# A first RMSNorm whose factor is applied to the results in PSUM instead of the operand

## The chip, the cores and the metric

The kernel is written in Bass for one core of one Trainium2 chip, with each engine's instruction stream written by hand. The metric is the device time of that core in microseconds, as the median of several executions.

## What is computed

Two blocks on x of 1 x 256 x 2048, all in float32. The part of the first that matters here, with `rmsnorm(x, g) = x * rsqrt(mean(x*x) + eps) * g` over the last axis:

```python
h = rmsnorm(x, norm_mix_pre)
proj = h @ w_in
xr, yr, q, k, v, g_rnn, g_attn = split(proj)   # 2048, 2048, 2048, 256, 256, 2048, 2048
xr = rg_lru(causal_depthwise_conv(xr, conv_w, conv_b), ...)   # gates, decay, scan over time
y_rnn = xr * gelu(yr)
q, k = rope(q), rope(k)
y_att = sliding_window_sink_attention(q, k, v, attn_sinks)
mix = sigmoid(g_rnn) * (y_rnn @ w_rnn_proj) + sigmoid(g_attn) * (y_att @ w_attn_proj)
x = x + rmsnorm(mix @ w_out, norm_mix_post)
h = rmsnorm(x, norm_mlp_pre); x = x + rmsnorm(relu(h @ w_mlp_up)**2 @ w_mlp_down, norm_mlp_post)
```

The second block has a norm, a wide input product, a differential attention, an S5 state-space branch and an output product.

## The kernel before, in words

**Products.** Each float32 product is three matmuls in fp32r: with the operand split into h_hi and h_lo and the weights into w_hi and w_lo, they are hi·hi, lo·hi and hi·lo, summed in PSUM. SP streams the weights in groups of two k-tiles by 512 columns (512 KB) into `raw`, a ring of four slots. ScalarE makes w_hi of a group (`split_hi`, L556), VectorE w_lo = raw - w_hi (`split_lo`, L1014). Eight groups are a unit, which fills `acc[u % 2]`, half of PSUM. `unit` on TensorE has two forms: by token (L1722 to L1724) and by feature (L1714 to L1717).

**Order.** Every engine walks the same list of units. `steps` on ScalarE and VectorE splits group j + 3 (`LEAD`) and then calls the hooks of step j: the unit's other work stands in these hooks, so a hook that waits holds up the splits behind it. `split_hi` of a group waits until TensorE is done with the group three before it (`pe_used`); SP's load waits for `lo_ready`; an accumulator comes free by `acc_free`.

**Start.** SP issues one DMA for x (L319), twelve for rows of parameters (L330), which land in `stg`, and then the weights. TensorE transposes the parameter rows (L1761, L1762), ScalarE copies them to `pt1` and `pt2`. ScalarE squares x (L581), VectorE and GpSimd make rstd of it (`mean_square`, POOL L432). For each of four chunks of 512 columns ScalarE writes x times rstd into `stg` (`h_chunk`, L594), TensorE transposes `stg` into `tps` (`turn`, L1737), ScalarE makes h_hi with the gain as scale (`evac_hi`, L574), VectorE h_lo (`evac_lo`, L1033). The first unit computes k and v (`U_KV`). Beside it and the next, VectorE computes the rotary angles, cosines, lambda, softplus and the rotation of k.

**Then** comes a loop of units for q and xr, in turn, with the attention in their hooks. xr goes from `acc` to `slab_d` on ScalarE (`xr_out`, L666).

**Recurrent units** (four, by feature, product yr; chunk c of 512 features in each). In their hooks: the gates (ScalarE L699, L702), decays (L712, L716) and a root (L721); on VectorE the decay (L1265 to L1267), the convolution of the next chunk (L1236, L1238) and the scan (`states`, L1272 to L1275). Behind a unit's steps ScalarE takes gelu of the accumulator (L729) into `slab_d`. In the next unit VectorE multiplies it with the scan's result (`y_product`, L1249) once `acc_free` says so; ScalarE makes the high part (`y_high`, L689), VectorE the low (`y_low`, L1254). POOL's queue loads the gate weights (L442).

**Mix units** follow: tanh of the gates from PSUM with scale 0.5 (L743), four times two units. The first block's second norm and the MLP are untouched. In the second block the norm's factor is already applied to results: rstd is turned into a row over all partitions by TensorE (`rstd_row`), copied (L825), and used as an operand (L1467, L1474).

In the names of tiles, `slab_dg_f` is `slab_d`, `slab_i_f` holds x, and `side` and `tps` are the two other parts of PSUM.

## Time and profile before

| | |
|---|---|
| median of 3 runs | 2541.09 us (2540.49 to 2541.24) |
| span of the profiled execution | 2539.6 us |
| its own time beside the span | the median lies 1.5 us above the span |
| TensorE busy | 2384.5 us, 94% |
| VectorE busy | 1483.3 us, 58% |
| ScalarE busy | 1206.1 us, 47% |
| GpSimd busy | 162.7 us, 6% |
| DMA | 410 MB, mean 161 GB/s |

The busy shares are means over the whole span. TensorE is nearly full overall, so the places to look at are those in which it is not, and there the waits tell which engine or transfer comes last. A "[idle <- releaser]" at a row's end is the time for which the engine stood before it and what ended that.

### The profile page before, as it was taken

What the parts mean: (1) busy time and instruction counts of PE and PEld (TensorE: products, weight loads), DVE (VectorE), ACT (ScalarE), POOL (GpSimd) and SP (SyncE); (2) the same over time, 40 slices, a digit from 0 to 9 for tenths busy, and PEclk for the clock granted to TensorE, in tenths of its full rate; (3) what the DMA queues carried; (4) which work ended last, traced back from release to release, by engine and by line L of the source; (5) the groups of instructions that cost most, each with busy time, mean ns of one, the idle gap of its engine ahead of it and who ended that gap; (6) DMA issues with size and microseconds to landing.
All of it is one profiled execution on the core that took longest, in us unless ns stands there. A gap on an engine that the chain in (4) does not pass through costs nothing.

```text
span 2539.6 us, 34016 instructions
## 1 busy us (share of the span) xinstructions
PE 2384.5 (94%) x11782; PEld 1962.7 (77%) x11782; DVE 1483.3 (58%) x1917; ACT 1206.1 (47%) x1746; POOL 162.7 (6%) x196
## 2 busy tenths in 40 slices
PE   5999888899999979999999999989999988898999
PEld 4888788888888868888888888879666657677887
DVE  3666557745454555545545555566778785665554
ACT  5444445544444444434444344354666754544443
POOL 2000000000000000000000000010433320010000
PEclk9999989999999989999999999999999998999999
DMA  5544324466666736666566666655333334445665
GB/s 178 162 132 125 114 86 132 153 195 190 190 191 191 255 127 191 187 195 188 186 189 189 191 188 188 191 151 174 107 108 99 107 108 125 140 140 156 185 189 166
DMA packets 209069, 410.00 MB, mean 161 GB/s; under 512 B 12960, under 2 KB 13248, under 8 KB 208192
## 3 DMA queue, kind: packets, MB, share of 16 engines
q1 hardware_dynamic: 206336, 398.64, 51.3%
q0 software_dynamic: 2624, 9.83, 1.3%
q8 instruction: 77, 1.26, 0.2%
q14 instruction: 32, 0.26, 0.0%
HBM read 406.33 MB, written 2.10 MB: 161 GB/s over the span
## 4 chain that ended last, share of the span: by engine, by line
PE 70%; issue 13%; DVE 8%; ACT 4%; POOL 3%; DMA 0%; SPq 0%; DVEq 0%; POOLq 0%; ACTq 0%
PE acc L1722 19%; PE acc L1724 19%; PE acc L1723 19%; PE acc L1714 3%; PE acc L1716 2%; PE acc L1717 2%; PE tps L1737 2%; DVE w_lo L1014 1%; PE side L1776 1%; ACT w_hi L556 1%; POOL k_t L474 1%; POOL t_low L473 1%; DVE stg L1238 1%; PE tps L1920 1%; DMA raw<-in_w_in_dram 0%
## 5 line engine op out<-in xcount | busy, mean ns | idle before, releaser
L1014 DVE TENSOR_TENSOR w_lo<-raw,w_hi 128x1024 fp32r<-128x1024 f32 x752 | 921.0, 1230 | 855.2 <-ACT w_hi L556 850.5
L556 ACT ACTIVATE w_hi<-raw 128x1024 fp32r<-128x1024 f32 x752 | 793.2, 1059 | 956.2 <-PE acc L1724 795.4
L1722 PE MATMUL acc<-w_hi,h_hi 128*128 128x512 f32 x1440 | 583.1, 405 | 22.9 <-DVE w_lo L1014 9.4
L1724 PE MATMUL acc<-w_hi,h_lo 128*128 128x512 f32 x1440 | 566.8, 394 | 0.0
L1723 PE MATMUL acc<-w_lo,h_hi 128*128 128x512 f32 x1440 | 566.5, 393 | 0.0
L1722 PEld LDWEIGHTS acc<-w_hi,h_hi 128*128 128x128 f32 x1440 | 274.2, 190 | 104.6 <-issue 33.4
L1724 PEld LDWEIGHTS acc<-w_hi,h_lo 128*128 128x128 f32 x1440 | 273.5, 190 | 59.6
L1723 PEld LDWEIGHTS acc<-w_lo,h_hi 128*128 128x128 f32 x1440 | 274.8, 191 | 52.8
L1722 PE MATMUL acc<-w_hi,slab_dg_r 128*128 128x512 f32 x768 | 299.4, 390 | 0.0
L1724 PE MATMUL acc<-w_hi,slab_dg_r 128*128 128x512 f32 x768 | 299.0, 389 | 0.0
L1723 PE MATMUL acc<-w_lo,slab_dg_r 128*128 128x512 f32 x768 | 298.8, 389 | 0.0
L1714 PE MATMUL acc<-h_hi,w_hi 128*128 128x256 f32 x768 | 225.5, 294 | 7.0 <-DVE w_lo L1014 7.0
L1716 PE MATMUL acc<-h_lo,w_hi 128*128 128x256 f32 x768 | 220.5, 287 | 0.0
L1717 PE MATMUL acc<-h_hi,w_lo 128*128 128x256 f32 x768 | 220.3, 287 | 0.0
L1723 PEld LDWEIGHTS acc<-w_lo,slab_dg_r 128*128 128x128 f32 x768 | 144.2, 188 | 29.9
L1724 PEld LDWEIGHTS acc<-w_hi,slab_dg_r 128*128 128x128 f32 x768 | 144.2, 188 | 29.8
L1722 PEld LDWEIGHTS acc<-w_hi,slab_dg_r 128*128 128x128 f32 x768 | 144.2, 188 | 29.8
L1714 PEld LDWEIGHTS acc<-h_hi,w_hi 128*128 128x128 f32 x768 | 150.7, 196 | 15.9 <-issue 15.6
L1716 PEld LDWEIGHTS acc<-h_lo,w_hi 128*128 128x128 f32 x768 | 150.8, 196 | 0.3
L1717 PEld LDWEIGHTS acc<-h_hi,w_lo 128*128 128x128 f32 x768 | 150.5, 196 | 0.0
L1722 PE MATMUL acc<-w_hi,slab_f_r 128*128 128x512 f32 x256 | 100.4, 392 | 0.0
L1724 PE MATMUL acc<-w_hi,slab_h_r 128*128 128x512 f32 x256 | 99.7, 389 | 0.0
(351 smaller groups left out, 2328.7 us busy)
## 6 DMA issues: line engine op xcount, KB each, us to landing
raw<-in_w_in_dram SPq DMA_DIRECT2D x328, 512.0 KB, 3.8
raw<-in_w_mlp_up_dram SPq DMA_DIRECT2D x128, 512.0 KB, 3.8
raw<-in_w_mlp_down_dram SPq DMA_DIRECT2D x128, 512.0 KB, 3.9
raw<-in_w_out_dram SPq DMA_DIRECT2D x64, 512.0 KB, 4.7
raw<-in_w_rnn_proj_dram SPq DMA_DIRECT2D x32, 512.0 KB, 4.2
raw<-in_w_attn_proj_dram SPq DMA_DIRECT2D x32, 512.0 KB, 4.8
raw<-in_w_proj_ssm_dram SPq DMA_DIRECT2D x16, 512.0 KB, 5.2
raw<-in_w_proj_att_dram SPq DMA_DIRECT2D x16, 512.0 KB, 4.4
```

The lines of the kernel that those rows point to most:

```text
L473: chain.link(pool.tensor_tensor(t_low[:, :], t_row, phi[:, 1, j:j + 1].broadcast_to([P, SEQ]), ALU.mult))
L474: chain.link(pool.tensor_tensor(f, f, k_round[:, j, :], ALU.subtract))
L556: nc.scalar.activation(w_hi[:, j % RING], raw[:, j % RING], ACT.Copy).then_inc(hi_ready, 1)
L1014: V.tensor_tensor(w_lo[:, j % RING], raw[:, j % RING], w_hi[:, j % RING].bitcast(F32), ALU.subtract)\
L1238: ins = V.scalar_tensor_tensor(xc4[:, m, late:], xr, w, xc4[:, m, late:], ALU.mult, ALU.add)
L1714: T.matmul(o, wh[:, c], hi[:, k, :], start=first and m % 2 == 0, stop=False, skip_group_check=True)
L1716: T.matmul(o, wh[:, c], lo[:, k, :], start=False, stop=False, skip_group_check=True)
L1717: ins = T.matmul(o, wl[:, c], hi[:, k, :], start=False, stop=last, skip_group_check=True)
L1722: T.matmul(o, hi[:, k, c], wh, start=first, stop=False)
L1723: T.matmul(o, hi[:, k, c], wl, start=False, stop=False)
L1724: ins = T.matmul(o, lo[:, k, c], wh, start=False, stop=last)
L1737: ins = T.transpose(tps[:, b * SEQ + t * P:b * SEQ + (t + 1) * P], stg[:, t, b * P:(b + 1) * P], ident[:, :])
```

## The change

h is no longer x·rstd·gain but x·gain, and rstd, one factor for each token, is applied to what comes out of PSUM.

- **Loads.** x comes in four DMAs of 512 columns (SP L338), alternating with the first three weight groups. The twelve parameter rows are issued from ScalarE's queue (L582).
- **Start.** TensorE transposes x itself as its chunks land, into two parts of PSUM in turn (`turn_x`), and ScalarE and VectorE evacuate with `x_high` (L595) and `x_low`. The squares follow in the hooks of steps 0 and 1 and rstd in the hook of step 2; the rotary hooks of ScalarE move back by one step, on VectorE cosines from 4 to 5.
- **k, q.** The cosines and sines are multiplied by rstd on VectorE, four small operations. **v** is copied in two with rstd as scale.
- **xr, yr.** They lie with tokens along the free axis. TensorE spreads rstd to a row in the second unit (hook 5), ScalarE copies it. xr leaves PSUM on VectorE, multiplied by the row. yr is multiplied by the row on VectorE behind the unit's steps (L1303), which frees the accumulator; gelu is taken in `slab_d` after it (L737), and `y_product` waits for `gelu_ready`.
- **Gates of the mix.** tanh takes half of rstd as its scale, one instruction for each half of the tokens.
- **POOL** starts the gate weights' loads when x's transposes are done (`tps_ready`).

SP at the start of the program; `raw` are the weights. Before:

```order
L319 DMA slab_i_f<-in_x_dram 128x2x2048
L330 DMA stg<-in_norm_mix_pre_dram 16x128
L330 DMA stg<-in_conv_w_dram 64x128
...
L330 DMA stg<-in_ssm_lambda_im_dram 32x128
L339 DMA raw<-in_w_in_dram 128x2x512 x4
```

Now:

```order
L338 DMA slab_i_f<-in_x_dram 128x2x512
L326 DMA raw<-in_w_in_dram 128x2x512
L338 DMA slab_i_f<-in_x_dram 128x2x512
L326 DMA raw<-in_w_in_dram 128x2x512
...
L326 DMA raw<-in_w_in_dram 128x2x512 [waits lo_ready] x4
```

The twelve rows have left SP, and x and the weights alternate.

VectorE from the scan of the second recurrent unit on. Before:

```order
L1275 SCALAR_TENSOR_TENSOR tmp<-tmp,slab_dg_f 128x256 [waits v_chain]
L1275 SCALAR_TENSOR_TENSOR tmp<-tmp,slab_dg_f 128x256 x3
L1014 TENSOR_TENSOR w_lo<-raw,w_hi 128x1024 [waits hi_ready] x2
L1249 TENSOR_TENSOR tmp<-slab_dg_f,tmp 128x1024 [waits y_ready,acc_free0]
L1014 TENSOR_TENSOR w_lo<-raw,w_hi 128x1024 [waits hi_ready]
```

Now (the row of rstd is called t_low here):

```order
L1287 SCALAR_TENSOR_TENSOR tmp<-tmp,slab_dg_f 128x256 [waits v_chain]
L1287 SCALAR_TENSOR_TENSOR tmp<-tmp,slab_dg_f 128x256 x3
L1005 TENSOR_TENSOR w_lo<-raw,w_hi 128x1024 [waits hi_ready]
L1303 TENSOR_TENSOR slab_dg_f<-acc,t_low 128x1024 [waits pe_used]
L1005 TENSOR_TENSOR w_lo<-raw,w_hi 128x1024 [waits hi_ready]
L1261 TENSOR_TENSOR tmp<-slab_dg_f,tmp 128x1024 [waits y_ready,gelu_ready]
L1005 TENSOR_TENSOR w_lo<-raw,w_hi 128x1024 [waits hi_ready]
```

The multiply stands between the two splits ahead of `y_product`, and waits for TensorE's end of the unit.

ScalarE at the same hand-over. Before:

```order
L556 ACTIVATE w_hi<-raw 128x1024 [waits pe_used,raw_landed2]
L729 ACT_TABLE_LOAD
L729 ACTIVATE slab_dg_f<-acc 128x1024 [waits pe_used]
L556 ACTIVATE w_hi<-raw 128x1024 [waits pe_used,raw_landed3]
L689 ACTIVATE slab_e_r<-tmp 128x1024 [waits y_ready]
```

Now:

```order
L549 ACTIVATE w_hi<-raw 128x1024 [waits pe_used,raw_landed2]
L737 ACT_TABLE_LOAD
L737 ACTIVATE slab_dg_f<-slab_dg_f 128x1024 [waits acc_free0]
L549 ACTIVATE w_hi<-raw 128x1024 [waits pe_used,raw_landed3]
L697 ACTIVATE slab_e_r<-tmp 128x1024 [waits y_ready]
```

gelu stands at its old place, but waits for VectorE's multiply instead of TensorE. The diff, cut to its core:

```diff
-            sp.dma_start(x_view, x_in).then_inc(x_landed, 16)
-            for rows, tile in ((FIRST_ROWS, 0), (SECOND_ROWS, 1)):
...
-                    sp.dma_start(stg[at:at + n, tile, 0:P], src).then_inc(rows_landed, 16)
...
-            unit(w_in, slice(o_k, o_k + NC), U_KV * S)
+            for c in range(NH):
+                at = slice(c * NC, (c + 1) * NC)
+                sp.dma_start(x_view[:, :, at], x_in[:, :, at]).then_inc(x_landed[c], 16)
+                if c < LEAD:
+                    load(w_in, slice(o_k, o_k + NC), 2 * c, U_KV * S + c, c)
+            for s in range(LEAD, S):
+                load(w_in, slice(o_k, o_k + NC), 2 * s, U_KV * S + s, s)
...
-                            pool.wait_ge(stg_ready, NH)
+                            pool.wait_ge(tps_ready, NH)
...
+            for rows, tile in ((FIRST_ROWS, 0), (SECOND_ROWS, 1)):
+                at = 0
+                for name, n in rows:
...
+                    act.dma_start(stg[at:at + n, tile, 0:P], src).then_inc(rows_landed, 16)
+                    at += n
 
             act.wait_ge(pt_ready, 1)
             nc.scalar.activation(pt1[:, :], tps[:, 0:P], ACT.Copy)
             nc.scalar.activation(pt2[:, :], tps[:, P:2 * P], ACT.Copy).then_inc(cols_ready, 1)
 
...
+            def x_high(c, t0, col):
+
+
...
+                for b in range(QPC):
+                    at = c * QPC + b
+                    ins = nc.scalar.activation(h_hi[:, at, :], x_bank(c, b), ACT.Copy, scale=col[:, at:at + 1])
+                ins.then_inc(tps_hi, 1)
...
+            def x_squares(c, first_x):
+                if first_x is None:
+                    act.wait_ge(x_landed[c], 16)
+                else:
+                    act.wait_ge(x_new, first_x + c + 1)
...
+                    ins = nc.scalar.activation(e_tok[:, t, c * NC:(c + 1) * NC], x_tok[:, t, c * NC:(c + 1) * NC],
+                                               ACT.Square, accum_out=ssq[:, t, c:c + 1])
...
                 act.wait_ge(ang_ready, 1)
...
-
+            def row_copy(index):
+                act.wait_ge(row_ready, index)
+                nc.scalar.activation(row[:, :], side[0][:, 0:SEQ], ACT.Copy).then_inc(row_copied, 1)
...
+            mix_gain = pt1[:, COL1["norm_mix_pre"]:COL1["norm_mix_pre"] + KT]
+            x_high(0, 0, mix_gain)
+            split_hi(None, 0, 0, 0)
+            split_hi(None, 0, 0, 1)
+            x_high(1, 0, mix_gain)
+            split_hi(None, 0, 0, 2)
+            hooks = {0: [lambda: x_squares(0, None), lambda: x_squares(1, None)], 1: [lambda: x_squares(2, None), lambda: x_squares(3, None)],
+                     4: [rotary_sines], 5: [exponentials]}
+            for c in range(2, NH):
+                x_high(c, 0, mix_gain)
+                steps(None, 0, U_KV * S, hooks, c - 1, start=c - 2)
+            steps(None, 0, U_KV * S, hooks, start=2)
+            unit_over(None, 0, U_KV * S)
             act.wait_ge(rstd_ready, 1)
-            first_unit(0, U_KV * S, pt1[:, COL1["norm_mix_pre"]:COL1["norm_mix_pre"] + KT],
-                       {3: [rotary_sines], 5: [exponentials]})
-            unit_over(None, 0, U_KV * S)
-            nc.scalar.activation(v_tok[:, :, :], tok(acc[0])[:, :, SEQ:2 * SEQ], ACT.Copy).then_inc(v_ready, 1)
+            for t in range(TT):
+                ins = nc.scalar.activation(v_tok[:, t, :], tok(acc[0])[:, t, SEQ:2 * SEQ], ACT.Copy, scale=rstd[:, t:t + 1])
+            ins.then_inc(v_ready, 1)
 
...
-                unit_over(i, 2 * S, (U_QX + 1 + 2 * c) * S)
-                settle()
-                nc.scalar.activation(slab_d[:, span(i, QPC, QPC * c, QPC), :], feat(acc[0]), ACT.Copy).then_inc(acc_free[0], 1)
...
-            steps(None, 0, U_QX * S, {5: [k_copy]})
+            steps(None, 0, U_QX * S, {3: [lambda: row_copy(1)], 5: [k_copy]})
...
-                beside_q[0] = [lambda: xr_out(i, 0)] + beside_q.get(0, [])
...
-                unit_over(None, 0, u * S)
-
-                nc.scalar.activation(slab_d[:, c * QPC:(c + 1) * QPC, :], feat(acc[u % 2]), ACT.Gelu_apprx_tanh)\
-                    .then_inc(acc_free[u % 2], 1)
+                act.wait_ge(acc_free[u % 2], u // 2 + 1)
+                at = slice(c * QPC, (c + 1) * QPC)
+                nc.scalar.activation(slab_d[:, at, :], slab_d[:, at, :], ACT.Gelu_apprx_tanh).then_inc(gelu_ready, 1)
             y_high(NH - 1)
 
 
...
-                    nc.scalar.activation(tmp[:, :, :], tok(acc[u % 2]), ACT.Tanh, scale=0.5).then_inc(acc_free[u % 2], 1)
+                    for t in range(TT):
+                        ins = nc.scalar.activation(tmp[:, t, :], tok(acc[u % 2])[:, t, :], ACT.Tanh, scale=half_rstd[:, t:t + 1])
+                    ins.then_inc(acc_free[u % 2], 1)
...
-            mean_square(1, 1)
...
+
+                dve.wait_ge(rstd_ready, 1)
+                chain.mark(V.tensor_scalar(half_rstd, rstd, 0.5, None, ALU.mult))
+                for t in range(TT):
+                    for b in (cosb, sinb):
+                        chain.mark(V.tensor_scalar(b[:, t, :], b[:, t, :], rstd[:, t:t + 1], None, ALU.mult))
 
                 dve.wait_ge(lam_landed, 160)
...
+            dve.wait_ge(cols_ready, 1)
+            x_low(0, H_X, mix_gain)
+            split_lo(None, 0, 0, 0)
+            split_lo(None, 0, 0, 1)
+            x_low(1, H_X, mix_gain)
+            split_lo(None, 0, 0, 2)
+            hooks = {2: [lambda: mean_square(NH, 1)], 3: [rotary_angles], 5: [cosines_and_lambda], 6: [softplus]}
+            for c in range(2, NH):
+                x_low(c, H_X, mix_gain)
+                steps(None, 0, U_KV * S, hooks, c - 1, start=c - 2)
+            steps(None, 0, U_KV * S, hooks, start=2)
+            dve.sem_inc(stg_ready, NH)
             dve.wait_ge(v_ready, 1)
...
+            def xr_out(i, c):
+                unit_over(i, 2 * S, (U_QX + 1 + 2 * c) * S)
+                rows_ = row[:, :].unsqueeze(1).broadcast_to([P, QPC, SEQ])
+                if i is not None:
+                    dve.wait_ge(row_copied, 1)
+                V.tensor_tensor(slab_d[:, span(i, QPC, QPC * c, QPC), :], feat(acc[0]), rows_, ALU.mult).then_inc(acc_free[0], 1)
+
...
+                    beside_q[0] = [lambda: xr_out(i, 0)] + beside_q.get(0, [])
...
+            xr_out(None, NH - 1)
...
-                dve.wait_ge(acc_free[(U_YR + c) % 2], (U_YR + c) // 2 + 1)
+                dve.wait_ge(gelu_ready, c + 1)
                 dve.wait_ge(y_ready, 2 * c + 1)
...
+                u = U_YR + c
+                unit_over(None, 0, u * S)
+                rows_ = row[:, :].unsqueeze(1).broadcast_to([P, QPC, SEQ])
+                V.tensor_tensor(slab_d[:, c * QPC:(c + 1) * QPC, :], feat(acc[u % 2]), rows_, ALU.mult).then_inc(acc_free[u % 2], 1)
             y_product(NH - 1)
...
             def turn_x(c, t0, first_x):
 
-                pe.wait_ge(x_new, first_x + c + 1)
-                pe.wait_ge(tps_free, t0 + max(c - 1, 0))
+                if first_x is None:
+                    pe.wait_ge(x_landed[c], 16)
+                else:
+                    pe.wait_ge(x_new, first_x + c + 1)
+                if t0 or c >= 2:
+                    pe.wait_ge(tps_free, t0 + max(c - 1, 0))
                 for t in range(TT):
...
+            def x_as_it_comes(c, t0, first_x):
+                pe.wait_ge(tps_free, t0 + c + 1)
+                if c < NH - 2:
+                    turn_x(c + 2, t0, first_x)
+
+            def rstd_row(index):
+
+                pe.wait_ge(rstd_ready, index)
+                for t in range(TT):
+                    ins = T.matmul(side[0][:, t * P:(t + 1) * P], rstd[:, t:t + 1].broadcast_to([P, P]), ident[:, :],
+                                   start=True, stop=True)
+                ins.then_inc(row_ready, 1)
+
+            for c in range(2):
+                turn_x(c, 0, None)
+            unit(None, 0, U_KV * S, 0, U_KV, h_hi, h_lo, before={4 * c // 2: [lambda c=c: x_as_it_comes(c, 0, None)] for c in range(NH)})
...
-            unit(None, 0, U_QX * S, 0, U_QX, h_hi, h_lo, hooks={9: [lambda: turn(None, 0, T_K)]})
+            unit(None, 0, U_QX * S, 0, U_QX, h_hi, h_lo, hooks={5: [lambda: rstd_row(1)], 9: [lambda: turn(None, 0, T_K)]})
```


## Rows read from the trace of the kernel before

**Rows 1.** Busy time by stretch of the span: TensorE, its loads, VectorE, ScalarE, GpSimd, clock, DMA

```profile
0.00:72.41 72.41, 39.46 (x166) 31.00 (x167) 32.88 (x93) 35.28 (x54) 16.82 (x36) 1.00 0.57 174
72.41:87.20 14.79, 14.79 (x70) 12.36 (x71) 8.25 (x7) 5.41 (x6) 0.00 (x0) 1.00 0.74 234
87.20:345.00 257.80, 241.15 (x1541) 209.94 (x1541) 153.65 (x347) 119.64 (x264) 0.00 (x0) 0.96 0.40 117
345.00:505.00 160.00, 144.06 (x973) 135.51 (x973) 113.31 (x148) 92.96 (x127) 5.76 (x8) 0.97 0.44 136
505.00:2539.60 2034.60, 1945.02 (x9037) 1573.85 (x9035) 1175.16 (x1324) 952.83 (x1297) 140.10 (x152) 0.98 0.55 168
```

**Rows 2.** Timeline of the start: start us, length us, engine, line, what, [idle before]

```profile
7.16 0.42 SPq L330 DMA_DIRECT2D stg<-in_ssm_lambda_im_dram  x1
...
14.16 0.45 PE L1762 MATMUL tps<-ident,stg 128*128 128x128 f32 x1 [14.16 <-DMA stg<-in_ssm_lambda_im_dram]
...
23.67 1.94 PE L1737 MATMUL tps<-ident,stg 128*128 128x128 f32 x8 [8.85 <-ACT stg L594]
...
27.25 1.66 DVE L1033 SCALAR_TENSOR_TENSOR h_lo<-tps,pt,h_hi 128x256 fp32r<-128x256 f32 x4 [3.69 <-ACT h_hi L574]
...
30.65 0.78 PE L1722 MATMUL acc<-w_hi,h_hi 128*128 128x512 f32 x1
...
34.21 0.63 PE L1724 MATMUL acc<-w_hi,h_lo 128*128 128x512 f32 x1
...
36.22 0.39 PE L1722 MATMUL acc<-w_hi,h_hi 128*128 128x512 f32 x1
...
47.31 1.66 DVE L1033 SCALAR_TENSOR_TENSOR h_lo<-tps,pt,h_hi 128x256 fp32r<-128x256 f32 x4 [3.58 <-ACT h_hi L574]
```

**Rows 3.** Timeline, VectorE's stream behind it and TensorE's wait for it

```profile
55.72 1.22 DVE L1014 TENSOR_TENSOR w_lo<-raw,w_hi 128x1024 fp32r<-128x1024 f32 x1 [1.42 <-ACT w_hi L556]
...
71.13 4.63 DVE L1014 TENSOR_TENSOR w_lo<-raw,w_hi 128x1024 fp32r<-128x1024 f32 x4 [0.15 <-DVE stg L1142]
...
72.41 0.50 PE L1722 MATMUL acc<-w_hi,h_hi 128*128 128x512 f32 x1 [1.55 <-DVE w_lo L1014]
```

**Rows 4.** Timeline of the recurrent units, second and third hand-over

```profile
392.62 1.22 DVE L1249 TENSOR_TENSOR tmp<-slab_dg_f,tmp 128x1024 f32<-128x1024 f32 x1
...
425.46 2.33 DVE L1014 TENSOR_TENSOR w_lo<-raw,w_hi 128x1024 fp32r<-128x1024 f32 x2
427.71 1.22 DVE L1249 TENSOR_TENSOR tmp<-slab_dg_f,tmp 128x1024 f32<-128x1024 f32 x1
...
414.79 1.02 ACT L729 ACTIVATE slab_dg_f<-acc 128x1024 f32<-128x1024 f32 x1
...
428.96 1.06 ACT L689 ACTIVATE slab_e_r<-tmp 128x1024 fp32r<-128x1024 f32 x1 [12.20 <-DVE tmp L1249]
...
451.50 0.55 PE L1714 MATMUL acc<-h_hi,w_hi 128*128 128x256 f32 x1 [3.43 <-DVE w_lo L1014]
```

**Rows 5.** DMA issues at 8.1, 8.6, 8.01, 8.53 and 9.06 us: KB, us to landing

```profile
raw<-in_w_in_dram SPq DMA_DIRECT2D x1, 512.0 KB, 11.8
...
raw<-in_w_in_dram SPq DMA_DIRECT2D x1, 512.0 KB, 12.6
...
slab_h_f<-in_lambda_k_dram POOLq DMA_DIRECT2D x1, 32.0 KB, 6.6
...
slab_h_f<-in_lambda_q_dram POOLq DMA_DIRECT2D x1, 32.0 KB, 8.0
...
slab_h_f<-in_lambda_k_dram POOLq DMA_DIRECT2D x1, 32.0 KB, 10.9
```

**Rows 6.** Groups by line, VectorE: the same multiply by the row, second block

```profile
L1474 DVE TENSOR_TENSOR stg<-acc,t_low 128x1024 f32<-128x1024 f32 x2 | 2.4, 1224 | 0.5 <-PE acc L1717 0.5
```

**Rows 7.** Timeline, TensorE's last wait behind the fourth recurrent unit

```profile
494.91 0.50 PE L1722 MATMUL acc<-w_hi,h_hi 128*128 128x512 f32 x1 [1.60 <-DVE w_lo L1014]
```

**Rows 8.** Busy time of the stretch 310 to 350 us, columns as in rows 1

```profile
310.00:350.00 40.00, 31.75 (x191) 29.30 (x190) 19.06 (x60) 14.30 (x33) 0.00 (x0) 0.79 0.17 45
```

More of the change, by code:

```diff
@@ L823, in _ @@
             steps(None, 0, G_U, start=2)
[L824 to L825 removed]
+            row_copy(2)
             steps(None, 0, G_U + S, {1: [s5_trig_]})
```

112 lines of the change are left out of this document (24 added, 88 removed).

## The prediction

> **What bounds the kernel now.** I read the time stretch by stretch first [rows 1]. From 505 us on TensorE is busy 1945.0 of 2034.6 us and the change touches only one ScalarE operation there, so the places to look at are the first 87 us and the stretch from 345 to 505 us. In the first 72.4 us TensorE is busy 39.5 us: that is where something can be won.
>
> The timeline of the start [rows 2] is a chain. The twelve parameter rows are issued on SP behind x, the last at 7.16 us, and TensorE's first two transposes start when they have landed, at 14.16 us. Then comes a chunk of x: eight transposes at 23.67, the end of its h_lo at 27.25 + 1.66 = 28.91, so 5.24 us for a chunk at the slow clock. Only after a second chunk's transposes does the first matmul start, at 30.65. Until 34.4 us matmuls follow each other every 0.43 us (a row of 0.63 us), later every 0.23 us (a row of 0.39 us): TensorE at 1.2 and then at 2.4 GHz, after a start from short bursts.
>
> From the last h_lo (47.31 + 1.66 = 48.97) VectorE is the bound [rows 3]: weight splits, rotary angles, lambda, softplus and the rotation of k stand in one stream, and TensorE's wait at 72.41 ends with the fourth group of the next unit, whose w_lo is the first of the four at 71.13. From 72.41 to 87.2 TensorE runs without a gap [rows 1], so what the end of that stream gains, the kernel gains.
>
> In the stretch from 345 us the four recurrent units are a ring of ScalarE and VectorE, not of TensorE [rows 4]. From one y_product (392.62) to the next (427.71) it is 35.1 us. TensorE works some 31.5 us of it and then waits for w_lo (3.43 us at 451.50). The ring: y_product, y_high on ScalarE (which had waited 12.20 us for it), splits, gates, decays, root, then VectorE's decay, convolution and scan, splits, y_product. The gelu at 414.79 stands outside it.
>
> **The start, part by part.** Removed from the path: the squares over all of x, the eight scalings of x into stg, and the wait of the first split and transposes for them. The transposes now need the parameter rows and x's chunk alone.
>
> When the rows land is the open term. They go out on ScalarE's queue, 12 at about 0.53 us each, so the last is issued near 7.1 us as before. In before, GpSimd's small transfers show what sharing costs [rows 5]: the one issued at 8.01 took 6.6 us, those at 8.53 and 9.06, which meet the 512 KB weight loads, took 8.0 and 10.9 us and landed at 16.5 and 20.0, while the loads issued at 8.1 and 8.6 landed at 19.9 and 21.2. A small transfer passed about once per load, not at once. Now eight such transfers (four of x, four of w) are issued by about 4.6 us. They take about 1.35 us each (19.9 to 21.2), with the small ones between them some 1.6 us: 1.5 + 8 x 1.6 = 14.3 us. Some eight of twelve rows have passed by then; the last four at 0.34 us each (twelve in 14.13 - 10.0 us behind x), and a landing, give 16 us. Bounds: 7.1 + 3.6 (the quickest load of the profile) = 10.7 us if they pass freely; 20 us if, like the transfer issued at 9.06, they take 10.9 us and more. I take 16, by the rows nearest to it. The Trainium skill (DMA: Bandwidth & Descriptors, Queues, rings and completion order) says the same: a DMA engine takes turns between the queues by packets of some 9 to 17 descriptors. It adds (Issuing engines are not separate DMA queues) that issuing from several engines saves only issue time, which speaks against this part; by it the rows land with the last of the eight transfers.
>
> From there: 1.5 us for two transposes and two copies (17.5); 5.24 us for chunk 0 (22.8); chunk 2's transposes, which now stand ahead of the unit, 1.9 us: first matmul at 24.7 us instead of 30.65. Two groups, 24 matmuls, take 5.5 us at 0.23 us each and about 1.2 us of slow clock (before: 2.2), chunk 3's transposes 1.0 us, its h_hi and h_lo 3.2 us: the last h_lo ends at 35.5 instead of 48.97, **13.5 us earlier**.
>
> VectorE's stream behind it took 72.3 - 48.97 = 23.3 us. It gains one w_lo of 1.15 us that used to stand ahead, 0.5 us of mean square, 0.85 us for half_rstd and the four scalings of cosine and sine, a wait of some 2.2 us for the w_hi that ScalarE now does behind squares of two chunks (3 us), 0.9 us of short waits, and loses the 1.4 us wait at 55.72: +4.2 us. So the matmul of 72.41 comes at 63.2 us: **the start gives 9.3 us**.
>
> At nothing: the transposes of rstd (0.3 us, while TensorE waits for VectorE anyway); the gate weights, now issued near 42 us (their unit is 300 us away); the split tanh of the mix units, 2 x 0.69 instead of 1.03 us, four times, covered by three groups of w_lo in stock (8 us); the v copy in two. If that cover were gone it would be 0.34 us each.
>
> **The xr copies** go from ScalarE (1.0 us) to VectorE (1.22 us, the same operation further on [rows 6]). In the loop VectorE is busy 153.65 of 257.80 us [rows 1] and the next user of that accumulator comes a unit later: zero. In the last unit the multiply stands ahead of the late `finish` calls, which wait for TensorE's products in any case: zero. If each did reach the path it would be 4 x 1.2 us.
>
> **The recurrent units.** Here the change adds to the ring. Before, gelu needed TensorE's unit alone, and was done 12 us before y_product. Now the multiply stands on VectorE behind the scan and the last split, since it is issued after them, and gelu, which waits for it, holds up ScalarE's next w_hi, on which VectorE's next w_lo waits, and behind that stands y_product. Before: w_lo, w_lo (2.25 us), y_product. After: w_lo 1.14, multiply 1.22, gelu 0.95, w_hi 1.07, w_lo 1.14 = 5.5 us. That is **+3.3 us** at each of three hand-overs. ScalarE's wait of 12.20 us hides none of it, because it ends with this same chain. At the fourth the w_hi stands behind y_high anyway: multiply and gelu alone, +2.2 us, and TensorE's wait at 494.91 is for what follows [rows 7]. Sum 3 x 3.3 + 2.2 = **+12.1 us**.
>
> **Sum:** -9.3 + 12.1 = +2.8 us. The profiled span of 2539.6 us becomes 2542.4; the median lies 1.5 us above that span, so 2541.1 + 2.8 = **2543.9 us**, slower by 0.11%. A measurement of this kernel can tell some 0.2%, 5.1 us, from no change.
>
> **Rivals.**
> 1. *The rows pass freely.* Landing at 10.7 us: the start gives 9.3 + 5.3 = 14.6, net -2.5: 2538.6 us. For: small transfers issued before 8 us took a steady 6.3 to 6.9 us. Against: the last two [rows 5].
> 2. *Slower: the rows are last of all.* Place: TensorE's first wait. If each turn of the engines costs 2 us, or the rows come after every load, they land at 20 us and the start gives 5.3: net +6.8, 2547.9 us. It decides from 18.4 us on (net +5.1).
> 3. *Slower: the clock joins the ring.* With some 8 us of waits in a unit of 38.4 us the granted clock could fall as it did at 310 to 350 us (0.79) [rows 8]. TensorE's 31.5 us were at 0.97 [rows 1], 30.5 at full clock, and become 38.6 at 0.79: the ring. At 0.70 they are 43.6, 5.2 us more in each of three units, net +18.4: 2559.5 us. It decides below 0.79.
> 4. *Faster: multiply and gelu fit into ScalarE's wait.* Net -9.3: 2531.8 us. It needs the multiply ahead of the scan, and the order of the code denies that.
> 5. *The change does not do what it says*: the first norm leaves the path only if the rows are not later than the norm was. They would have to land at 25 us.
>
> **How the numbers follow.** My forecast 0.50, rival 1 0.24, rival 2 0.13, rival 3 0.05, rival 4 0.05, others 0.03. Faster by over 0.2% (under 2536.0): rival 4 and the edge of rival 1, 0.09. Slower by over 0.2% (over 2546.2): rivals 2 and 3 and some, 0.18. Within: 0.73. The range runs from the low bound of the landing (rival 1) to its high bound (rival 2), 2538.0 to 2548.5, and leaves out 3, 4 and the rest.
>
> **What would show it.** First transposes at 16 us (10.7: rival 1; 20: rival 2); first matmul near 24.7; TensorE's last wait for w_lo of the second unit ending at 63. From y_product to y_product 38.4 us, with w_lo, multiply, gelu, w_hi, w_lo in a row ahead of it; 35.1 us would refute me. The stretch from 505 us unchanged within 1 us. I am wrong if the recurrent stretch grows by less than 8 us, or if the start is bound by x or w and not by the rows.

## The result, and the profile after

| | before | changed |
|---|---|---|
| median | 2540.49 us (9 runs, 2537.54 to 2543.27) | 2546.34 us (9 runs, 2545.19 to 2548.16) |
| ratio | | 1.0023, 95% interval 1.0013 to 1.0033 |
| span of the profiled execution | 2539.6 us | 2543.9 us |
| mean granted clock | 0.978 | 0.973 |

The change makes the kernel slower by 5.9 us of medians (0.23%), 4.3 us between the two profiled spans. The forecast was 2543.9 us, 2538.0 to 2548.5, and most likely no change that can be told. The time lies in the range, but a little beyond the 0.2% (2546.2 us) that counted as none, an outcome to which the forecast gave 0.18. What became of the two halves can be read well, because at each place the two traces can be compared in time.

Busy time of the changed kernel in the stretches of [rows 1], columns as there:

```profile
0.00:72.41 72.41, 50.10 (x221) 41.16 (x222) 39.34 (x104) 35.81 (x64) 17.71 (x36) 0.95 0.71 213
72.41:87.20 14.79, 13.86 (x96) 12.49 (x95) 10.49 (x14) 5.46 (x6) 0.00 (x0) 1.00 0.54 168
87.20:345.00 257.80, 239.87 (x1538) 208.62 (x1537) 161.41 (x361) 116.34 (x259) 0.00 (x0) 0.96 0.38 114
345.00:505.00 160.00, 136.09 (x887) 127.00 (x886) 105.09 (x130) 87.17 (x121) 5.77 (x8) 0.93 0.41 125
505.00:2543.90 2038.90, 1950.45 (x9053) 1578.29 (x9051) 1177.27 (x1325) 955.99 (x1307) 140.36 (x152) 0.98 0.54 168
```

TensorE is busy 10.6 us longer by 72.41 us than before, and 8.0 us less in the recurrent stretch. In each row "(x...)" is the number of instructions, and the last three columns are the granted clock, the busy share of the DMA engines and GB/s.

The start, the changed kernel's timeline (it answers to [rows 2, 3]):

```profile
7.09 0.63 ACTq L582 DMA_DIRECT2D stg<-in_ssm_lambda_im_dram  x1
...
15.57 0.45 PE L1766 MATMUL tps<-ident,stg 128*128 128x128 f32 x1 [15.57 <-DMA stg<-in_ssm_lambda_im_dram]
...
23.54 0.78 PE L1730 MATMUL acc<-w_hi,h_hi 128*128 128x512 f32 x1
...
32.96 1.66 DVE L1050 SCALAR_TENSOR_TENSOR h_lo<-side,pt,h_hi 128x256 fp32r<-128x256 f32 x4 [3.17 <-ACT h_hi L595]
...
57.23 0.80 PE L1730 MATMUL acc<-w_hi,h_hi 128*128 128x512 f32 x1 [2.68 <-DVE w_lo L1005]
...
85.74 0.92 PE L1795 MATMUL side<-k_c,slab_dg_f 64*128 64x128 f32 x4 [0.93 <-ACT slab_dg_f L650]
```

The last row is the attention's first scores; before, they came here:

```profile
96.34 0.92 PE L1776 MATMUL side<-k_c,slab_dg_f 64*128 64x128 f32 x4 [0.93 <-ACT slab_dg_f L635]
```

The parameter rows have landed at 15.57 us (16 forecast), the first matmul of the product starts at 23.54 (24.7), the last h_lo ends at 34.6 (35.5), and the first scores are 10.6 us earlier.

A hand-over between recurrent units in the changed kernel, VectorE, ScalarE and TensorE (before: [rows 4]):

```profile
418.50 1.20 DVE L1005 TENSOR_TENSOR w_lo<-raw,w_hi 128x1024 fp32r<-128x1024 f32 x1
419.62 1.22 DVE L1303 TENSOR_TENSOR slab_dg_f<-acc,t_low 128x1024 f32<-128x1024 f32 x1
422.91 1.22 DVE L1005 TENSOR_TENSOR w_lo<-raw,w_hi 128x1024 fp32r<-128x1024 f32 x1 [2.07 <-ACT w_hi L549]
424.05 1.22 DVE L1261 TENSOR_TENSOR tmp<-slab_dg_f,tmp 128x1024 f32<-128x1024 f32 x1
...
420.87 1.06 ACT L737 ACTIVATE slab_dg_f<-slab_dg_f 128x1024 f32<-128x1024 f32 x1 [13.05 <-DVE slab_dg_f L1303]
421.83 1.04 ACT L549 ACTIVATE w_hi<-raw 128x1024 fp32r<-128x1024 f32 x1
...
447.83 0.55 PE L1722 MATMUL acc<-h_hi,w_hi 128*128 128x256 f32 x1 [4.81 <-DVE w_lo L1005]
...
462.42 1.22 DVE L1261 TENSOR_TENSOR tmp<-slab_dg_f,tmp 128x1024 f32<-128x1024 f32 x1
```

Split, multiply, gelu, w_hi, split, y_product stand in a row as the forecast had them, and from one y_product to the next it is 38.37 us (38.4 forecast, 35.1 before). ScalarE still waits 13 us, now for the multiply and ahead of gelu. TensorE's granted clock does fall in this ring, to 0.67 over 405 to 415 us and 0.66 over 444 to 454 us, where the lowest such stretches of before read 0.81 to 0.87 (385 to 395, 415 to 424 and 444 to 454 us); TensorE's waits (4.81 us here) take it up, and the period stays.

The way out of the last recurrent unit, TensorE, and the clock behind its wait, in the changed kernel (before: [rows 7]):

```profile
489.92 0.50 PE L1730 MATMUL acc<-w_hi,h_hi 128*128 128x512 f32 x1 [1.32 <-DVE w_lo L1005]
...
496.88 0.66 PE L1730 MATMUL acc<-w_hi,h_hi 128*128 128x512 f32 x1 [3.95 <-DVE w_lo L1005]
497.35 0.63 PE L1731 MATMUL acc<-w_lo,h_hi 128*128 128x512 f32 x1
...
500.63 0.40 PE L1730 MATMUL acc<-w_hi,h_hi 128*128 128x512 f32 x1
```

```profile
496.80:500.00 3.20, 3.12 (x8) 2.44 (x9) 3.20 (x4) 1.43 (x2) 0.00 (x0) 0.54 0.57 166
```

The wait of 1.60 us has become 3.95, and behind it eight matmuls run at 1.2 GHz (0.43 us apart) and not at 2.4 GHz (0.23 us): 1.6 us that the forecast did not have. Before, the granted clock was 1.00 there. From the end of this wait to the first tanh of the mix it is 15.53 us, and was 13.93.

Put together, by how much later (+) or earlier (-) the changed kernel is at the same piece of work: first scores -10.6; fourth y_product (492.12 against 490.15) +2.0; first tanh of the mix (512.41 against 508.84) +3.6; last tanh (819.76 against 816.19, the first half of it in the changed kernel) +3.6; first multiply by a row in the second block (1705.43 against 1700.88) +4.6; end +4.3. From the first tanh to the end it is 0.7 us longer, within the 1 us that the forecast allowed for that stretch. The first y_product (385.67 against 392.62) is at -6.95, with the first 3.3 us of the ring in it, so the lead on entry was -10.25. (From the first scores to this y_product it is 299.93 us, and 296.65 in the first experiment, which takes the ring's part out: 3.28 us.)

### The profile page after: what moved, and what is told of

Read it like the earlier page. It is cut to its first block, busy times and chain, and to the rows that moved or that the text cites. A ratio compares the mean times of both kernels' runs of the same rounds, so it can differ in the third digit from the quotient of the medians.

```text
span 2543.9 us, 34049 instructions
## 1 busy us (share of the span) xinstructions
PE 2390.4 (94%) x11786; PEld 1967.6 (77%) x11786; DVE 1493.6 (59%) x1931; ACT 1200.8 (47%) x1756; POOL 163.8 (6%) x196
## 4 chain that ended last, share of the span: by engine, by line
PE 71%; issue 13%; DVE 8%; ACT 4%; POOL 3%; DMA 0%; ACTq 0%; DVEq 0%; POOLq 0%
PE acc L1730 19%; PE acc L1731 19%; PE acc L1732 19%; PE acc L1722 3%; PE acc L1725 3%; PE acc L1724 3%; PE tps L1745 1%; DVE w_lo L1005 1%; ACT w_hi L549 1%; PE side L1795 1%; POOL k_t L467 1%; POOL t_low L466 1%; DVE stg L1250 1%; PE tps L1926 1%; POOL att L490 0%
## 5 line engine op out<-in xcount | busy, mean ns | idle before, releaser
L1730 PE MATMUL acc<-w_hi,h_hi 128*128 128x512 f32 x1440 | 584.3, 406 | 24.3 <-DVE w_lo L1005 10.6
```

The lines of the kernel that those rows point to most:

```text
L1730: T.matmul(o, hi[:, k, c], wh, start=first, stop=False)
```

## The experiments

All are edits of the changed kernel. Each went beside runs of the kernel before on the same chip, whose median was 2540.7 to 2541.5 us. The experiments ran on different chips in part, and the medians of before alone differ by 1.0 us between them, so between two experiments' medians a difference of that size says nothing. Diffs are cut at "...".

**1. The recurrent part undone.** The factor of yr is left out.

```diff
...
-                act.wait_ge(acc_free[u % 2], u // 2 + 1)
+                unit_over(None, 0, u * S)
-                nc.scalar.activation(slab_d[:, at, :], slab_d[:, at, :], ACT.Gelu_apprx_tanh).then_inc(gelu_ready, 1)
+                nc.scalar.activation(slab_d[:, at, :], feat(acc[u % 2]), ACT.Gelu_apprx_tanh).then_inc(acc_free[u % 2], 1)
...
-                V.tensor_tensor(slab_d[:, c * QPC:(c + 1) * QPC, :], feat(acc[u % 2]), rows_, ALU.mult).then_inc(acc_free[u % 2], 1)
...
```

> The changed kernel with its part in the recurrent units undone: gelu is taken straight from the accumulator on ScalarE, VectorE's multiply and the factor of yr are left out. My theory (the recurrent units cost the change 12.2 us by the ring and another 1.6 us by the slow clock behind TensorE's wait of 3.95 us): from one y_product to the next 35.1 us as before, the wait at the last hand-over back near 1.6 us with the clock at 1.00 behind it, a profiled span of 2543.9 - 13.8 = 2530.1 us, 10 us under before. Rival (the lead of the start would be lost behind the recurrent units in any case, because there the weight loads come last, as at 498.7 us of before): span 2535 us or more, with ScalarE waiting longer for loads.

Measured: 2532.88 us, ratio to before 0.9964 (0.995 to 0.9978), span 2530.4. Two y_products and the way out:

```profile
417.84 1.22 DVE L1261 TENSOR_TENSOR tmp<-slab_dg_f,tmp 128x1024 f32<-128x1024 f32 x1
452.92 1.22 DVE L1261 TENSOR_TENSOR tmp<-slab_dg_f,tmp 128x1024 f32<-128x1024 f32 x1
...
485.03 0.50 PE L1726 MATMUL acc<-w_hi,h_hi 128*128 128x512 f32 x1 [1.61 <-DVE w_lo L1005]
```

The period is 35.08 us, the wait 1.61 us. The whole loss is in the recurrent part: by medians 13.5 us (2546.34 - 2532.88), between the two spans 13.5 too, and 13.8 was expected before the run. The rival, a lead that cannot pass the recurrent units, is out: the other parts of the change alone are 8 us faster than before.

**2. The multiply ahead of the scan.** In the hook of `states`, with the wait for the unit's end:

```diff
...
-                             5: conv_b, 6: [states]}
+                             5: conv_b, 6: [by_row, states]}
...
```

> VectorE's multiply of yr by the row stands ahead of the scan instead of behind the unit's last split, so that gelu runs on ScalarE beside the scan. My theory (two things are on the ring, the multiply itself, 1.2 us, and the gelu with the w_hi behind it, 2.1 us): the period from y_product to y_product falls from 38.4 to 36.3 us, the last hand-over gains 1.1, span 2543.9 - 3 x 2.1 - 1.1 = 2536.5 us, and 2534.9 if the clock stays at 1.00 behind the last hand-over. Rival (TensorE ends the unit only after VectorE gets there, so the wait moves with the multiply): period 38 us or more, span 2543 us.

Measured: 2536.6 us, 0.9977 (0.9968 to 0.9986), span 2534.8.

```profile
420.11 1.22 DVE L1261 TENSOR_TENSOR tmp<-slab_dg_f,tmp 128x1024 f32<-128x1024 f32 x1
456.32 1.21 DVE L1261 TENSOR_TENSOR tmp<-slab_dg_f,tmp 128x1024 f32<-128x1024 f32 x1
...
484.95 0.79 PE L1732 MATMUL acc<-w_hi,h_hi 128*128 128x512 f32 x1 [2.45 <-DVE w_lo L1005]
...
486.39 0.63 PE L1732 MATMUL acc<-w_hi,h_hi 128*128 128x512 f32 x1
...
489.56 0.50 PE L1732 MATMUL acc<-w_hi,h_hi 128*128 128x512 f32 x1
```

The period is 36.21 us, 1.13 over before: of the 3.3 us the multiply is 1.1, and gelu and the w_hi behind it are 2.2. The way out takes 18.7 us from the last y_product to the first tanh, as before (508.84 - 490.15), and 20.3 in the changed kernel. The clock falls here too: behind the wait of 2.45 us seven matmuls are 0.43 us apart or more, and the granted clock is 0.53 over 484.9 to 488.5 us. But TensorE then reaches the next group (489.56) without a wait, where before it stood 1.60 us [rows 7]; so the slow matmuls cost nothing. Moved by a few lines, the same work is faster than before.

**3. The multiply on GpSimd.** ScalarE copies the accumulator, GpSimd multiplies in SBUF, ScalarE takes gelu:

```diff
...
+                nc.scalar.activation(slab_d[:, at, :], feat(acc[u % 2]), ACT.Copy).then_inc(acc_free[u % 2], 1)
+                act.wait_ge(yr_scaled, c + 1)
...
+                        pool.tensor_tensor(slab_d[:, at, :], slab_d[:, at, :],
+                                           t_low[:, :].unsqueeze(1).broadcast_to([P, QPC, SEQ]), ALU.mult).then_inc(yr_scaled, 1)
...
```

> The multiply of yr by the row is taken off VectorE: ScalarE copies the accumulator to SBUF (0.95 us), GpSimd multiplies there (by the rows of 128 x 256, 0.76 to 1.17 us each, 3 to 4.7 us), ScalarE takes gelu. The 6 us lie in ScalarE's wait of 12.2 us ahead of y_high. My theory: period 35.1 us, last hand-over at most 1.5 us later than in before, span 2530 to 2532 us, faster than before by 8 to 10 us. Rival (GpSimd's operation slows VectorE's beside it): VectorE's convolution and splits get longer by 1 us and more for each unit, span 2535 us or more.

Measured: 2547.44 us, 1.0025 (1.0016 to 1.0034), span 2544.5: a miss, and it has two causes. GpSimd, VectorE and ScalarE:

```profile
385.96 2.40 POOL L435 TENSOR_TENSOR slab_dg_f<-slab_dg_f,t_low 128x1024 f32<-128x1024 f32 x1 [31.30 <-PE side L1859]
...
413.40 2.34 POOL L435 TENSOR_TENSOR slab_dg_f<-slab_dg_f,t_low 128x1024 f32<-128x1024 f32 x1 [22.20 <-ACT slab_dg_f L751]
...
412.27 3.75 DVE L1266 SCALAR_TENSOR_TENSOR stg<-slab_dg_f,pt,stg 128x255 f32<-128x255 f32 x4
...
388.38 1.06 ACT L753 ACTIVATE slab_dg_f<-slab_dg_f 128x1024 f32<-128x1024 f32 x1 [18.43 <-POOL slab_dg_f L435]
```

The first multiply was queued on GpSimd behind the wait for the gates of the second unit (`rg_done`), a fault of my placing; the first y_product comes 8.8 us later for it (391.56 against 382.76 in the first experiment). The rest is the rival: beside GpSimd's 2.34 us four convolution steps of VectorE take 3.75 us instead of 1.67, and the period is 37.2 us (391.56, 428.72, 465.90), 2.1 over before. That is dearer than the 1.1 us of the multiply on VectorE itself. The Trainium skill (GPSIMD Engine Reference, Specifications) says that GpSimd shares its SBUF interfaces with VectorE, with contention for VectorE's instructions with two SBUF inputs, as these are. The trace agrees, with 2.08 us lost beside 2.34; that it is these interfaces no run here shows by itself.

**4. w_hi ahead of gelu.**

```diff
...
-                    steps(None, 0, u * S, {0: [lambda: y_high(c - 1)], 2: [gates], 3: [decays], 4: [root]})
+                    steps(None, 0, u * S, {0: [lambda: gelu(c - 1), lambda: y_high(c - 1)], 2: [gates], 3: [decays], 4: [root]})
...
```

> ScalarE makes the next unit's w_hi ahead of gelu instead of behind it, in the first three recurrent units; VectorE's multiply stays where it is. My theory (the same split of the 3.3 us, seen from ScalarE's side): the split on VectorE no longer waits for gelu, which runs beside it, so the period falls from 38.4 to about 36.3 us; the last hand-over and the clock behind it stay; span 2543.9 - 3 x 2.1 = 2537.6 us. Rival (the multiply alone makes the 3.3 us, gelu and w_hi are hidden): period 38.4 us, span 2543.9 us.

Measured: 2540.16 us, 0.9996 (0.9987 to 1.0005), 6.2 us under the changed kernel's median (6.3 expected). The profiled span, 2534.6, is 3 us better than expected, but that execution was the fastest of the eleven (2536.45 us); its start was 2 us earlier (see below), so the median is the better measure of the edit.

```profile
417.69 1.22 DVE L1265 TENSOR_TENSOR tmp<-slab_dg_f,tmp 128x1024 f32<-128x1024 f32 x1
453.98 1.23 DVE L1265 TENSOR_TENSOR tmp<-slab_dg_f,tmp 128x1024 f32<-128x1024 f32 x1
...
488.43 0.80 PE L1734 MATMUL acc<-w_hi,h_hi 128*128 128x512 f32 x1 [3.95 <-DVE w_lo L1009]
```

The period is 36.29 us: gelu off the way, the multiply left, the same split from the other engine. The last hand-over, which the edit leaves, keeps its wait of 3.95 us and its 20.1 us to the first tanh.

**5. The parameter rows back on SP, behind x and w.** The loop of twelve DMAs moves from ScalarE to SP:

```diff
...
-                    act.dma_start(stg[at:at + n, tile, 0:P], src).then_inc(rows_landed, 16)
+                    sp.dma_start(stg[at:at + n, tile, 0:P], src).then_inc(rows_landed, 16)
...
```

> The changed kernel with the twelve parameter rows back on SP's queue, behind the eight transfers of x and the weights. In five profiles of the changed start the rows landed at 15.0 to 17.4 us, and TensorE's first scores of the attention came 68.8 or 70.2 to 70.6 us after them. My theory (one queue is served in order, so the rows are last; they are issued until 11.3 us and land 6 us after that): rows at 17.5 to 18.5 us, first scores at 87.7 to 89.1, span 2 to 3 us over the changed kernel's 2543.9. Rival (which engine issues changes nothing, the rows come when all bytes before them have come): rows at 15 to 17.4 us, span and median as the changed kernel's.

Measured: 2553.09 us, 1.0046 (1.0032 to 1.006), span 2551.2.

```profile
10.98 2.69 SPq L351 DMA_DIRECT2D stg<-in_b_glu_dram  x1
13.71 1.46 SPq L351 DMA_DIRECT2D stg<-in_ssm_lambda_re_dram  x1
15.22 1.44 SPq L351 DMA_DIRECT2D stg<-in_ssm_lambda_im_dram  x1
...
22.04 0.45 PE L1766 MATMUL tps<-ident,stg 128*128 128x128 f32 x1 [22.04 <-DMA stg<-in_ssm_lambda_im_dram]
```

The direction is mine, the size is not: the rows land at 22.04 us. The last three issues take 1.4 to 2.7 us each; on ScalarE's queue the last three took 0.34 to 0.63. The 6.5 us are found again one for one: first y_product 391.95 against 385.67 us, median +6.75. The Trainium skill (DMA: Bandwidth & Descriptors, Issuing engines are not separate DMA queues) says that a second issuing engine saves issue time only. That much the trace bears out: the last row goes out 8.1 us later and lands 6.5 us later. But I had taken the rule to speak against this part, and the issue time on a queue with 3.5 MB ahead was what the part was worth.

**6. The weights held back until the rows have landed,** behind two chunks of x (1 MB):

```diff
...
+                if c == 1:
+                    sp.wait_ge(rows_landed, 16 * 12)
+                    load(w_in, slice(o_k, o_k + NC), 0, U_KV * S, 0)
+                elif c in (2, 3):
+                    load(w_in, slice(o_k, o_k + NC), 2 * (c - 1), U_KV * S + c - 1, c - 1)
...
```

> The changed kernel with SP waiting for the parameter rows behind the first two chunks of x, so that the rows share the engines with 1 MB instead of 4 MB; the weights and the other chunks follow in turn (w, x, w, x, w). My theory (the rows' landing sets the start, one for one): rows at 10.7 to 12 us, first scores 70.2 to 70.6 us after them plus 1 to 2 us because w0 and w1 now land late, so at 82 to 84.5 us instead of 85.7, span 2540 to 2543 us. Rival (VectorE's stream behind it or the weights set the start whatever the rows do): first scores at 85 to 86.5 us or later, span 2543.9 or more.

Measured: 2545.57 us, 1.0014 (1.0005 to 1.0023), span 2543.8.

```profile
10.44 0.45 PE L1771 MATMUL tps<-ident,stg 128*128 128x128 f32 x1 [10.44 <-DMA stg<-in_ssm_lambda_im_dram]
...
20.36 1.94 PE L1764 MATMUL tps<-ident,slab_i_f 128*128 128x128 f32 x8 [5.05 <-DMA slab_i_f<-in_x_dram]
...
18.93 1.06 ACT L554 ACTIVATE w_hi<-raw 128x1024 fp32r<-128x1024 f32 x1 [3.73 <-DMA raw<-in_w_in_dram]
```

The rows are 5 us earlier, and TensorE then waits 5.05 us for x, ScalarE 3.73 for w: first scores at 85.23 us, where I had expected 82 to 84.5: a miss. The granted clock behind that wait is 0.50 from 20 to 26 us, which adds to it. With the rows out of the way the loads are the bound, so it is a bound right behind the rows'.

**7. The gate weights issued later.**

```diff
...
+                        if c == 0:
+                            pool.wait_ge(pe_used, 3 * S)
...
```

> The changed kernel with GpSimd's eight loads of the gate weights (2 MB) held until TensorE has done three units; in the changed kernel they are issued from 40.5 to 46.3 us, and the weight loads of that time take 7 to 7.8 us to land instead of 3.8, with waits of ScalarE for loads from 52.6 to 67.9 us. My theory (VectorE's stream is the bound there, so the collision is hidden): first scores 70.2 to 70.6 us after the rows' landing as before, span within 0.5 us. Rival (the collision is on the path): ScalarE's waits for loads go and the first scores come 1 to 2 us earlier against the rows' landing.

Measured: 2546.35 us, 1.0018 (1.0009 to 1.0027), the changed kernel's median. One of ScalarE's waits for loads is left (1.58 us at 54.64), yet the first scores come 71.2 us after the rows (15.42, 86.58), not earlier. So the rival is out, and the collision of loads near 45 us was hidden, as forecast. The profiled span, 2546.2 us, is not within 0.5 us of the changed kernel's. Of the 2.3 us, 1.0 is lost between rows and scores, and that is TensorE's clock: behind the wait for the second unit's w_lo (57.23 us in the changed kernel, 56.56 here) 13 matmuls are slow, and 6 in the changed kernel. Seven more at 0.2 us each are 1.4 us, and two fewer at 20 to 30 us give back 0.4.

```profile
56.56 0.79 PE L1732 MATMUL acc<-w_hi,h_hi 128*128 128x512 f32 x1 [2.67 <-DVE w_lo L1007]
...
61.42 0.63 PE L1734 MATMUL acc<-w_hi,h_lo 128*128 128x512 f32 x1
```

Another 1.0 us lies between scores and first y_product (387.46), where the eight loads now fall into the loop (issued from 110 us on); that they are its cause is not shown. The medians show neither.

**8. Held back behind 2 MB,** two chunks of x and two weight groups:

```diff
...
                 at = slice(c * NC, (c + 1) * NC)
+                if c == 2:
+                    sp.wait_ge(rows_landed, 16 * 12)
...
```

> The changed kernel with SP waiting for the parameter rows after two chunks of x and two weight groups (2 MB); the other two chunks and w2, w3 follow. With 1 MB ahead the rows landed at 10.4 us, with 3.5 to 4 MB at 15.0 to 17.4, which is 1.7 us for each MB. My theory: rows at 12 to 12.5 us; w0 and w1 have landed by then and x's third chunk, needed 6.7 us after the rows, lands in time; first scores 68.8 to 70.6 us after the rows, so at 81 to 83 us (85.7 in the changed kernel), median 3 us under the changed kernel's 2546.3, so 2543. Rival (as with 1 MB: the transfers held back come late themselves and eat it): waits of TensorE or ScalarE for x or w between 16 and 25 us, median within 1 us of 2546.

Measured: 2545.76 us, 1.0016 (1.0006 to 1.0025), span 2544.9. Rows at 13.07 us, no wait for x or w between 16 and 25 us, first scores at 83.68 (70.6 behind the rows), first tanh 1.9 us before the changed kernel's; the median was only 0.6 us lower, where I had expected 3. So it was run once more beside the changed kernel:

> The changed kernel itself, on the same chip as the next run. Theory (the time of the span behind the mix units, in which no instruction was changed, differs by some 3 us from profile to profile, 884 to 888 us from the last tanh to the first multiply of the second block): first tanh of the mix at 512 to 514.5 us, median 5 to 6.5 us over before.

> SP's wait for the rows after 2 MB, once more, beside the changed kernel. In the first run the first tanh came 1.9 us earlier than in the changed kernel, and the median was 0.6 us lower, where I had expected 3; on top of the multiply ahead of the scan it gave 2.7. Theory (the rows land 2.5 us earlier and this stays to the end, medians differ by what else varies): median 2 to 3 us under the changed kernel of this call. Rival (the lead is lost behind the start): median within 1 us of it.

Measured: the changed kernel 2546.92 us (1.002, 1.0011 to 1.0029), the held one 2544.39 us (1.0008, 0.9999 to 1.0017), rows at 15.41 and 13.45. Here the difference is 2.5 us. The traces show where part of the lead is lost. The first y_product is 2.7 and 3.5 us earlier (383.02 against 385.67, 382.60 against 386.09), the first tanh of the mix only 1.9 and 2.0 us: behind the wait of 3.9 us more matmuls were slow (from the last y_product to the first tanh it is 21.06 and 21.59 us, and 20.29 and 20.06 in the two profiles of the changed kernel). Then comes a long stretch in which no instruction was changed, from the last tanh of the mix to the first multiply by a row in the second block. It takes 884.7 us in before, 885.7 and 885.4 us in the changed kernel, 888.2 and 886.9 us in the held one, and 884.7 to 888.5 us over all thirteen profiles of the changed kernel and its edits. So these 1 to 3 us are not the held kernel's own; they differ from profile to profile, and why, I don't know. Nor can the one profile of before say whether the change has a part in it.

**9. Both edits together,** the multiply ahead of the scan and the 2 MB:

> Both edits together: VectorE's multiply ahead of the scan, and SP's wait for the rows after 2 MB. The two places are 300 us apart, so my theory is that they add: median 2536.6 of the first alone less 3 us, 2533.5 us, 0.3% under before. Rival (a lead of the start is lost before the recurrent units): median 2536 to 2537 us, with the first y_product no earlier than 383.9 us.

Measured: 2533.93 us, 0.9971 (0.9959 to 0.9983), span 2532.6, periods of 36.21 us, first y_product at 379.98. They add (2.7 us under the first alone), and this version is faster than both kernels, 6.8 us under before.

**10. The other copies back.** xr is copied on ScalarE, tanh and v are one instruction each, and their factor is left out:

```diff
...
-                    for t in range(TT):
-                        ins = nc.scalar.activation(tmp[:, t, :], tok(acc[u % 2])[:, t, :], ACT.Tanh, scale=half_rstd[:, t:t + 1])
-                    ins.then_inc(acc_free[u % 2], 1)
+                    nc.scalar.activation(tmp[:, :, :], tok(acc[u % 2]), ACT.Tanh, scale=0.5).then_inc(acc_free[u % 2], 1)
...
```

> The changed kernel with the copies of xr back on ScalarE and the tanh of the mix units and the copy of v as one instruction each; the norm's factor of xr, v and the gates is left out. The forecast took these three at nothing. My theory: 0.3 us between the first scores and the scan and 0.5 to 0.7 us in the mix units, as the two traces differ there, at most 1 us in all, median 2545.3 to 2546.3 us, the last tanh of the mix units as far from the first as in before (307.4 us; 307.9 in the changed kernel). Rival (the multiply of xr on VectorE delays its splits in each turn): 4 x 1.2 us, median 2541.5 us, and the first y_product 4 us earlier against the rows' landing (370 us).

Measured: 2545.34 us, 1.0019 (1.001 to 1.0028), 1.0 us under the changed kernel. All tanh of the mix, their times and the first and last start:

```profile
L755 ACT ACTIVATE tmp<-acc x8: 1027/1029/1029, 512.0 to 819.4; 128x1024 f32<-128x1024 f32 x8
```

The first and the last pair of the changed kernel:

```profile
512.41 1.27 ACT L751 ACTIVATE tmp<-acc,small 128x512 f32<-128x512 f32 x2 [1.60 <-PE acc L1732]
...
819.76 1.27 ACT L751 ACTIVATE tmp<-acc,small 128x512 f32<-128x512 f32 x2 [1.60 <-PE acc L1732]
```

From the start of the first to the start of the last it is 307.35 us in the changed kernel, 307.35 in before (816.19 - 508.84) and 307.35 here (819.36 - 512.01). Splitting the tanh costs nothing on the way. (The 307.9 us of the expectation ran to the start of the last tanh's second half.) The first y_product is 0.4 us earlier, with the rows at the same 15.56 us, and the last tanh is 0.4 us earlier too: that is what xr costs. Four multiplies of 1.2 us would have been 4.8, so the rival is out. The 1.0 us between the medians is more than the traces show and too little to be told.

**The start across all profiles.** When the rows landed, when the first scores came, and the granted clock of two stretches, 20 to 30 us and 50 to 70 us (with the rows on SP 27 to 37 and 57 to 77):

| run | rows | scores | scores - rows | clock, 20 to 30 | clock, 50 to 70 |
|---|---|---|---|---|---|
| changed | 15.57 | 85.74 | 70.2 | 0.83 | 0.91 |
| changed, again | 15.41 | 85.54 | 70.1 | 0.83 | 0.91 |
| other copies back | 15.56 | 85.70 | 70.1 | 0.83 | 0.91 |
| multiply ahead of scan | 16.22 | 86.76 | 70.5 | 0.83 | 0.91 |
| multiply on GpSimd | 15.03 | 85.61 | 70.6 | 0.83 | 0.91 |
| rows on SP | 22.04 | 92.61 | 70.6 | 0.83 | 0.91 |
| held, 2 MB | 13.07 | 83.68 | 70.6 | 0.83 | 0.91 |
| recurrent part undone | 17.36 | 86.11 | 68.8 | 1.00 | 0.91 |
| w_hi ahead of gelu | 15.01 | 83.77 | 68.8 | 1.00 | 1.00 |
| held, 2 MB, again | 13.45 | 82.19 | 68.7 | 1.00 | 1.00 |
| both edits | 13.03 | 81.78 | 68.8 | 1.00 | 1.00 |
| gate weights later | 15.42 | 86.58 | 71.2 | 1.00 | 0.83 |
| held, 1 MB | 10.44 | 85.23 | 74.8 | 0.69 | 0.91 |

Two things set the start. Where x and the weights are there in time (all but the last line), the rows' landing goes through one for one over 9 us, and TensorE's clock adds 1.4 to 2.4 us or not. The stretch of 20 to 30 us in the changed kernel and in the fourth experiment:

```profile
20.00:30.00 10.00, 7.74 (x31) 6.58 (x32) 9.33 (x16) 9.48 (x21) 0.00 (x0) 0.83 0.54 171
```

```profile
20.00:30.00 10.00, 8.30 (x44) 6.97 (x45) 9.22 (x16) 9.52 (x22) 0.00 (x0) 1.00 0.57 178
```

31 matmuls in the one, 44 in the other, with the same code up to there; the held kernel, run twice, shows both. Part of what differs between executions of one kernel is this. The column of the first stretch does not tell it all: with the gate weights later it reads 1.00, yet the first three matmuls are 0.43 us apart or more, and the larger loss comes at 50 to 70 us. Here the distance between matmuls is the surer sign.

## Why the prediction was right

- **The start's term** (-9.3 us) was -10.6 at the first scores and -10.25 on entry to the recurrent units. The open value, the rows' landing, was taken as 16 us and was 15.57, and 15.0 to 17.4 in all eight profiles with this order of transfers; both bounds (10.7, 20) were wrong for this kernel but real: 10.44 with the loads held, 22.04 on SP. Rival 1 needed 10.7 and rival 2 from 18.4 on. (The quickest weight load of before took 3.4 us, not the 3.6 of the low bound, which changes nothing.) That 16 us was so near is in part luck: its terms (1.6 us for a large transfer, eight rows passed by then) were not measured one by one. Of the 0.9 us by which the gain on entry was larger, 0.4 is the landing. The rest is not separated; TensorE, not VectorE's split, is the bound from 57.23 us on, where I had its last wait at 63.2. That step was wrong in place, and cost little.
- **"Which speaks against this part"**, said of the Trainium skill's rule on issuing engines and the rows on ScalarE's queue, does not hold: in the fifth experiment, without that part, the start's gain shrinks by 6.5 us. The sum went by the rows of the profile and did not use it.
- **The ring's term** (+12.1 us): 38.37 us from y_product to y_product where 38.4 was forecast, and from entry to the fourth y_product -10.25 to +1.97 = +12.2. The first and the second experiment show cause and parts: 1.1 us for the multiply, 2.2 for gelu and w_hi, three times, and 2.3 at the last. "ScalarE's wait hides none of it" holds, as does that rival 4 needs the multiply ahead of the scan; even there the multiply's own 1.1 us stays, so that rival's "-9.3" was too good.
- **The clock** (rival 3) did not set the ring's pace: it fell to 0.66 and 0.67 over 10 us of a unit, TensorE still waited 4.81 us, and the period was 38.4. Its cost came where the forecast had only "TensorE's wait at 494.91 is for what follows": that wait grew by the 2.3 us of the fourth hand-over to 3.95, the clock fell to 1.2 GHz behind it, +1.6 us. In all nine profiles with a wait of 3.9 us there it is 20.1 to 21.6 us from the last y_product to the first tanh, in the four experiments with a shorter one 18.7 to 18.8, as in before. This is the term missing from the sum.
- **"At nothing"**: the split tanh is at nothing, 307.35 us from first to last as in before. xr costs 0.4 us where I had zero; its cover is not quite free.
- **The sum**: -10.25 + 12.2 + 1.6 = +3.6 us at the first and at the last tanh of the mix, and 0.7 us more in untouched code behind it, which makes the +4.3 us between the two spans. The medians differ by 5.85 (3.3 to 8.4). That is twice the forecast's +2.8 us. Of the 3.0 us between the two, the traces explain 0.8: the clock's 1.6 and the ring's 0.1, less 0.95 for the start. Not explained are 0.7 us in untouched code and 1.5 between spans and medians (the profiled execution of the changed kernel was itself 0.7 us under its median). The mechanism came true part by part; that the time lies in the range owes something to its width, and that it went beyond 2546.2 us had neither of the two reasons given for it (rivals 2 and 3).

## What to carry to other kernels

Factoring a scale out of an operand pays where the norm stood on the path, and costs where the results are read by an engine in a ring; the place of that one instruction in its engine's order decides: behind the scan it cost 3.3 us a unit, ahead of it 1.1. Ask of a moved operation not only what it takes but what is queued behind whoever waits for it: two thirds of the 3.3 us were gelu and the weight split behind it. At the start, the smallest transfers can be the ones that everything waits for; give them a queue of their own, and few bytes to share the engines with, but not so few that the large loads come last (sixth experiment).
